# Moving the norm's root and shift behind the product: two extra columns, rows of 784 words, in a two-layer diffusion block

## The reference, cut to what matters

```python
def rms_norm(x, w):
    y = x * lax.rsqrt(jnp.mean(x * x, axis=-1, keepdims=True) + NORM_EPS) * w
def modulate(h, shift, scale):
    return h * (1.0 + scale) + shift
def swiglu(h, w_in, w_out):
    gate, up = jnp.split(h @ w_in, 2, axis=-1)
    return (jax.nn.silu(gate) * up) @ w_out

mod = (silu(c) @ w_ada[layer] + b_ada[layer])      # 9 vectors of 1024, one set for latent, one for context
h = h + 0.5 * lm[2] * swiglu(modulate(rms_norm(h, norm_w[layer, 0]), lm[0], lm[1]), ffn_w_in[layer, 0], ffn_w_out[layer, 0])
y, yc = token_mix(modulate(rms_norm(h, norm_w[layer, 1]), lm[3], lm[4]), ...)   # first product: @ w_in, 2048 columns
```

## Time and profile before

| | |
|---|---|
| time, median of 3 runs | 2741.3 us (2737.53 to 2744.84) |
| the profiled execution | 2739.12 us, of it the span 2737.2 us |
| mean granted TensorE clock | 0.992 |
| busy: PE / PEld / DVE / ACT / POOL | 2664.7 / 2290.5 / 1521.2 / 692.3 / 93.7 us |
| instructions in the span | 42267, of them 15515 matmuls |
| DMA read | 313.73 MB, 115 GB/s over the span |

### The profile page before, as it was taken

How to read it: one execution, slowest core, us unless ns; L and a number is a source line. 1 busy time by engine, 2 the same in 40 slices (tenths; PEclk the granted TensorE clock), 3 DMA queues, 4 the chain that set the end, 5 groups by cost and what they waited for, 6 DMA issues and landing times.

```text
span 2737.2 us, 42267 instructions
## 1 busy us (share of the span) xinstructions
PE 2664.7 (97%) x15515; PEld 2290.5 (84%) x15515; DVE 1521.2 (56%) x2621; ACT 692.3 (25%) x1075; POOL 93.7 (3%) x211
## 2 busy tenths in 40 slices
PE   7999999999999999999999999999999989999998
PEld 4888888888877888888888888888887877888886
DVE  5776477534376477626763677247536465543333
ACT  4111111122256221111111311111113345422222
POOL 0000000000034000000000000000000022000000
PEclk8999999999999999999999999999999999999999
DMA  7877477412200177536762577257422200233332
GB/s 228 198 184 185 113 184 184 125 50 79 54 17 2 54 165 185 146 86 159 184 161 58 123 184 175 71 140 184 126 70 84 69 26 17 81 96 100 91 110 81
DMA packets 485795, 316.98 MB, mean 116 GB/s; under 512 B 30588, under 2 KB 483664, under 8 KB 485712
## 3 DMA queue, kind: packets, MB, share of 16 engines
q1 hardware_dynamic: 485712, 315.88, 45.2%
HBM read 313.73 MB, written 2.10 MB: 115 GB/s over the span
## 4 chain that ended last, share of the span: by engine, by line
PE 91%; DVE 4%; ACT 2%; issue 1%; POOL 1%; DMA 0%; SPq 0%; DVEq 0%; ACTq 0%; POOLq 0%
PE pg L709 79%; PE pg L776 4%; PE p L1047 1%; PE pn L1030 1%; PE pg L986 1%; PE p L724 1%; DVE xlo L1640 1%; DVE tnorm L1632 1%; PE pg L867 1%; ACT whi L1155 0%; DVE wlo L1493 0%; PE pg L991 0%; DVE probT L1847 0%; DVE mx L1854 0%; ACT xhi L1244 0%
## 5 line engine op out<-in xcount | busy, mean ns | idle before, releaser
L709 PE MATMUL pg<-xhi,whi 128*128 128x512 f32 (+1 forms) x2856 | 794.5, 347 | 4.1 <-DVE wlo L1493 4.0
L709 PE MATMUL pg<-xhi,wlo 128*128 128x512 f32 (+1 forms) x2856 | 788.6, 344 | 0.0
L709 PE MATMUL pg<-xlo,whi 128*128 128x512 f32 (+1 forms) x2856 | 787.1, 344 | 0.0
L1155 ACT CAST whi<-raw 128x1024 fp32r<-128x1024 f32 (+1 forms) x288 | 321.8, 1118 | 1060.2 <-PE pg L709 1045.9
L1493 DVE TENSOR_TENSOR wlo<-raw,whi 128x1024 fp32r<-128x1024 f32 (+1 forms) x288 | 377.6, 1311 | 350.5 <-ACT whi L1155 347.8
L709 PEld LDWEIGHTS pg<-xhi,whi 128*128 128x128 f32 x2856 | 451.3, 188 | 72.6 <-DVE wlo L1493 5.9
L709 PEld LDWEIGHTS pg<-xlo,whi 128*128 128x128 f32 x2856 | 450.4, 188 | 69.3
L709 PEld LDWEIGHTS pg<-xhi,wlo 128*128 128x128 f32 x2856 | 450.4, 188 | 68.9
L1577 DVE SCALAR_TENSOR_TENSOR part<-ada,cond,part 128x256 f32<-128x256 f32 x960 | 465.3, 485 | 32.7
L1703 DVE SCALAR_TENSOR_TENSOR h<-pg,gcol,h 128x512 f32 (+1 forms) x118 | 71.4, 639 | 442.3 <-PE pg L709 437.5
L709 PE MATMUL pg<-ahi,whi 128*128 128x512 f32 x1100 | 306.1, 346 | 0.0
(11 more groups left out here) (212 smaller groups left out, 1983.4 us busy)
## 6 DMA issues: line engine op xcount, KB each, us to landing
ada<-in_w_ada SPq DMA_DIRECT2D x512, 256.0 KB, 4.2
raw<-in_ffn_w_in SPq DMA_DIRECT2D x176, 512.0 KB, 3.9
raw<-in_ffn_w_out SPq DMA_DIRECT2D x64, 704.0 KB, 4.5
raw<-in_w_in SPq DMA_DIRECT2D x24, 512.0 KB, 3.8
ada_first<-in_w_ada SPq DMA_DIRECT2D x8, 1024.0 KB, 11.9
raw<-in_w_in SPq DMA_DIRECT2D x16, 256.0 KB, 3.5
raw<-in_w_o SPq DMA_DIRECT2D x16, 256.0 KB, 2.8
raw<-in_w_o SPq DMA_DIRECT2D x32, 128.0 KB, 2.9
```

Source lines behind the costliest of these rows:

```text
L709: last = nc.tensor.matmul(pg[s][:, p0:p1], w[:, s, k], v[:, k, p0:p1], start=(k == 0 and n == 0), stop=(k == kt - 1 and n == 2))
L1155: nc.scalar.copy(whi[:, s, 0:nk], raw[:, s, 0:nk]).then_inc(s_whi[s], 1)
```

## The change

Norms 0, 1, 2 and 3 (`POST`) are applied after the product. `xhi`, `xlo` hold A·h, without r and s; two more columns of them (768, 769) hold s for latent and context. So the second matmul of each pair has 258 columns, and rows of `xhi`, `xlo` have 784 words. At the eviction DVE multiplies `pg[s]` by `rstd` and copies the two columns W^T s to `gbias`; ACT adds them as its bias. Norms 4 and 5 stay as they were. After the `out` phases before norms 1 and 3 (`EARLY_K` = 6) the tiles k = 0 to 5 are written during the last pair. In the opening the squares are taken from the token rows with an accumulated sum on ACT; DVE makes a diagonal of them (`ident` times `ssq`) for the same `square_sums`; PE has these ahead of the first modulation. In norm 1 `rstd` goes to `rstd_w`, since `rope_sb` is loaded over `rstd`, and that load also waits for the root.

```diff
+        XB, XW = TOK + 2, TOK + 16
-        xhi = place("xhi", [P, KD, TOK], f32r, start["xhi"])
+        xhi = place("xhi", [P, KD, XW], f32r, start["xhi"])
...
+        POST = (0, 1, 2, 3)
+        EARLY_K = {1: KD - 2, 3: KD - 2}
+        def product_columns(m, t):
+            return TOK + 2 if m in POST else t
...
                         if n == (6 if late_context(i) else 4):
                             sp.wait_ge(s_xn, xn_count(m, 1, KD - 1))
+                            sp.wait_ge(s_r, 2 * m + 2)
...
-                parts = [(0, SEQ)] + ([(SEQ, TOK)] if t == TOK else [])
+                parts = [(0, SEQ)] + ([(SEQ, t)] if t > SEQ else [])
...
-                        if part_ == 0 and (s, k) == (0, 1):
+                        if part_ == 0 and (s, k) == (order[-1] if m in POST else (0, 1)):
                             square_sums(m, 1)
...
             def opening_pair(i):
-                first_modulation(0)
                 square_sums(0, 0)
                 square_sums(0, 1)
+                first_modulation(0)
                 first_fold(0)
...
+            for tt in range(TOK // P):
+                act.wait_ge(s_x[tt // 2], 32)
...
+                nc.scalar.activation(sqjunk[tt % 2][:, :], xtok[:, tt, :], ACT.Square, accum_out=ssq[:, tt:tt + 1]
+                                     ).then_inc(s_sq, 1 if tt < TOK // P - 1 else KD - TOK // P + 1)
...
+            def scaled_hi(m, part_, k):
+                nc.scalar.activation(xhi[:, k, p0:p1], h[:, k, p0:p1], ACT.Identity, scale=acol[:, k, v:v + 1]
+                                     ).then_inc(s_xh, 1)
+            def shift_columns_hi(m, k0, k1):
+                nc.scalar.copy(xhi[:, k0:k1, TOK:XB], mod[:, shift + k0:shift + k1, 0:2])
...
+                if m == 0:
+                    for q in range(KD // 2):
+                        if q == 2:
+                            copy_first(2)
+                        act.wait_ge(s_coef, coef_count(0, 2 * q))
+                        shift_columns_hi(0, 2 * q, 2 * q + 2)
+                        for k in (2 * q, 2 * q + 1):
+                            scaled_hi(0, 0, k)
+                            scaled_hi(0, 1, k)
+                        if q == 1:
+                            nc.scalar.preload_act_table_set("natural_log_exp_and_others")
+                            root(0)
+                            root(1)
+                    return
+                if m in POST:
+                    if phases[i][0] == "wo":
+                        act.wait_ge(s_coef, coef_count(m, 0))
+                        for k in range(4):
+                            scaled_hi(m, 0, k)
+                        split_hi(i + 1, 0, 0)
+                        square_part(i, 1, 0)
+                        for k in range(4, KD):
+                            scaled_hi(m, 0, k)
+                        split_hi(i + 1, 1, 0)
...
+                        if m in POST:
+                            split_hi(nxt, 0, jn)
+                            act.wait_ge(s_free[0], read_value(i, f))
+                            nc.scalar.activation(gate[:, 0:SEQ], gate[:, 0:SEQ], ACT.Silu, bias=gbias[:, 0:1])
+                            nc.scalar.activation(gate[:, SEQ:TOK], gate[:, SEQ:TOK], ACT.Silu, bias=gbias[:, 1:2]
+                                                 ).then_inc(s_gd, 1)
+                            split_hi(nxt, 1, jn)
+                            return
...
+                        if m in POST:
+                            dve.wait_ge(s_unit[0], f + (j0 + 1))
+                            nc.vector.tensor_tensor(gate[:, :], pg[0][:, 0:TOK], rstd[:, :], ALU.mult)
+                            nc.vector.tensor_copy(gbias[:, 0:2], pg[0][:, TOK:XB]).then_inc(s_free[0], 1)
                         split_lo(nxt, 0, jn)
...
+                        if m in POST:
+                            nc.vector.tensor_copy(gbias[:, 2:4], pg[1][:, TOK:XB])
+                            nc.vector.tensor_tensor(u, pg[1][:, 0:TOK], rstd[:, :], ALU.mult).then_inc(s_free[1], 1)
+                            dve.wait_ge(s_gd, gate_count(m, hf, f))
+                            for v, (p0, p1) in enumerate(((0, SEQ), (SEQ, TOK))):
+                                last = nc.vector.scalar_tensor_tensor(gate[:, p0:p1], u[:, p0:p1],
+                                                                      gbias[:, 2 + v:3 + v], gate[:, p0:p1],
+                                                                      ALU.add, ALU.mult)
...
+                        if m in POST:
+                            nc.vector.tensor_tensor(z[:, n, :], pg[s][:, 0:TOK], rstd_w[:, :], ALU.mult)
+                            nc.vector.tensor_scalar(gbias[:, 2 * s:2 * s + 2], pg[s][:, TOK:XB], tile_scale(n), None,
+                                                    ALU.mult).then_inc(s_free[s], 1)
+                            split_lo(nxt, s, jn)
```

More of the change, by code:

```diff
@@ L125, in transformer @@
         h = place("h", [P, KD, TOK], f32, start["h"])
-        xhi = place("xhi", [P, KD, TOK], f32r, start["xhi"])
-        xlo = place("xlo", [P, KD, TOK], f32r, start["xlo"])
+        xhi = place("xhi", [P, KD, XW], f32r, start["xhi"])
+        xlo = place("xlo", [P, KD, XW], f32r, start["xlo"])
         ahi = place("ahi", [P, HALF, TOK], f32r, start["ahi"])
@@ L141, in transformer @@
         gate = place("gate", [P, TOK], f32, m0 + TOK * 4)
+        up = place("up", [P, HALF, TOK], f32, start["alo"])
+        gbias = sb("gbias", [P, 4])
+        sqjunk = [place(f"sqjunk{b}", [P, D], f32, at) for b, at in enumerate((m0 + 3 * TOK * 4, m0 + 4096))]
+        ssq = place("ssq", [P, TOK // P], f32, m0 + 3 * TOK * 4 + D * 4)
         xtok = place("xtok", [P, TOK // P, D], f32, start["alo"])
@@ L159, in transformer @@
               for tt in range(TOK // P)]
-        ysum = [place(f"ysum{ft}", [P, TOK], f32, start["xlo"] + ft * TOK * 4) for ft in range(2)]
-        ysin = [place(f"ysin{ft}", [P, TOK], f32, x0 + ft * TOK * 4) for ft in range(2)]
+        ysum = [place(f"ysum{ft}", [P, TOK], f32, start["xlo"] + ft * XS) for ft in range(2)]
+        ysin = [place(f"ysin{ft}", [P, TOK], f32, x0 + ft * XS) for ft in range(2)]
         vret = place("vret", [P, TOK // P, 2 * P], f32, m0)
         xlo0 = start["xlo"]
-        kdk = place("kdk", [P, TOK // P, RH, 2, HD], f32, xlo0 + 4 * TOK * 4)
-        qd = [place(f"qd{hd}", [P, TOK], f32, x0 + k * TOK * 4) for hd, k in enumerate((2, 3, 6, 7))]
+        kdk = place("kdk", [P, TOK // P, RH, 2, HD], f32, xlo0 + 4 * XS)
+        qd = [place(f"qd{hd}", [P, TOK], f32, x0 + k * XS) for hd, k in enumerate((2, 3, 6, 7))]
         qdt = place("qdt", [P, RH, P], f32, start["ada"] + 2 * TOK * 4)
@@ L1082, in _ @@
                         with pe.Fori(a, e) as f:
-                            unit(i, 0, f, xhi, xlo, t)
-                            unit(i, 1, f, xhi, xlo, t)
+                            unit(i, 0, f, xhi, xlo, product_columns(m, t))
+                            unit(i, 1, f, xhi, xlo, product_columns(m, t))
                             if b is not None:
@@ L1666, in norm @@
                         read_first(q)
-                        scaled(0, 2 * q)
-                        scaled(1, 2 * q)
-                        low(0, 2 * q)
-                        scaled(0, 2 * q + 1)
-                        low(1, 2 * q)
-                        scaled(1, 2 * q + 1)
+                        scaled_low(0, 0, 2 * q)
+                        shift_columns_low(0, 2 * q, 2 * q + 2)
+                        scaled_low(0, 1, 2 * q)
+                        scaled_low(0, 0, 2 * q + 1)
                         if q == 0:
                             copy_first(1)
-                        low(0, 2 * q + 1)
-                        low(1, 2 * q + 1)
+                        scaled_low(0, 1, 2 * q + 1)
+                    return
+                if m in POST:
+                    if phases[i][0] == "wo":
+                        for k in range(3):
+                            scaled_low(m, 0, k)
+                        add_part(i, 1, 0)
+                        split_lo(i + 1, 0, 0)
+                        scaled_low(m, 0, 3)
+                        sum_part(m, 1, 0)
+                        for k in (4, 5):
+                            scaled_low(m, 0, k)
+                        add_part(i, 1, 1)
+                        split_lo(i + 1, 1, 0)
+                        for k in (6, 7):
+                            scaled_low(m, 0, k)
+                        sum_part(m, 1, 1)
+                        shift_columns_low(m, 0, KD)
+                        for k in range(KD):
+                            scaled_low(m, 1, k)
+                    else:
+                        split_lo(i + 1, 0, 0)
+                        sum_part(m, 1, 0)
+                        add_part(i, 1, 1)
+                        scaled_low(m, 1, KD - 2)
+                        split_lo(i + 1, 1, 0)
+                        sum_part(m, 1, 1)
+                        scaled_low(m, 1, KD - 1)
```

(8 more changed lines are left out.)

185 lines of the change are left out of this document (135 added, 50 removed).

## The result

The kernel after takes 2750.35 us (median of 7 runs, 2749.2 to 2754.04), the kernel before 2741.3 us in the same comparison (2737.53 to 2744.84): **ratio 1.0033, 95% interval 1.0022 to 1.0044**. It is slower by 9 us, just past the 0.3% taken as the bound (the interval lies on both sides of it), where the forecast was 2725.5 us with a range to 2736. The profiled execution took 2749.2 us (span 2747.4). Every gain that was forecast is there, and more than their sum has gone into the pace of TensorE's products.

The account below looks back on a forecast made before the run. PE, busy in 97% of the span, was taken as the bound. Terms +3.0 − 5.5 − 4.4 − 5.6 − 3.4 − 0.5 + 0.6 gave −15.8 us, moving the median 2741.3 to 2725.5 us, range 2716 to 2736.

Parts of the forecast that it names:

- Norms 1, 2 and 3: Where these norms meet the next product, PE's waits for `xlo` tiles and splits shrink: −5.5, −5.6 and −4.4 us.
- the opening: Earlier sums of squares give −3.4 us, the opening pair −0.5; first product near 61.7 instead of 65.6.
- PE's clock no longer falls there: Sign at the norms: the forecast is wrong if the granted clock still falls at norms 1 and 2.
- the first mixing: ACT's query copies start some 0.6 us later, delaying DVE's decay product: +0.6 us, between 0 and 1.2.
- the eviction is hidden: In 132 FFN and 16 mixing units, DVE's added 2.5 us per step fits its idle time: 0 us.
- one gap left in the step: Sign in FFN steps: DVE idle about 1.3 us ahead of the up tile, under 0.5 ahead of slot 0's split.
- Rival D: DVE becomes the bound of the FFN steps, all 61 stretch by 0.4 us, +24 − 16: 2750 us; chance 0.06.
- the sign that I had set: The forecast is wrong if a steady FFN step is longer than 17.2 us; 17.14 expected instead of 17.10.
- Two more columns: 3552 second matmuls grow from 256 to 258 columns, 0.83 ns each: +3.0 us on PE, ends 0 and 3.5.
- Rival C: The two columns are free under the weight load: −18.8 us, 2722.5 us; chance 0.12.

Follow-up runs that it names:

- Run 14: Changed kernel with rows of 832 words and 256 columns in the second matmul, the shift left out of the products; 2722.26 us, ratio 0.9929.
- run 5: Changed kernel with rows of 800 words instead of 784, 258 columns kept; 2754.19 us, ratio 1.005.
- run 6: Changed kernel with rows of 784 words, but 256 columns instead of 258 in the second matmul; 2743.44 us, ratio 1.0011.
- run 7: Changed kernel with rows of 800 words and 256 columns in the second matmul; 2746.22 us, ratio 1.0021.
- run 13: Changed kernel with rows of 832 words, 258 columns kept; 2738.74 us, ratio 0.9998.
- Run 18: Changed kernel, 832-word rows, shift packed in `xhi`, order whi·xhi (260 columns), wlo·xhi (258), whi·xlo (256); 2716.95 us, ratio 0.9912.
- run 2: Kernel before with 512 bytes left free behind `xhi` and again behind `xlo`, rows still 768 words; 2740.69 us, ratio 0.9995.
- run 4: Kernel before with everything moved by 384 bytes together; 2741.14 us, ratio 1.0002.
- run 10: Kernel before with `xhi`, `xlo` moved by 256 bytes against everything else; 2739.46 us, ratio 0.9996.
- run 12: Kernel before with everything moved by 64 bytes together; 2741.91 us, ratio 1.0004.
- run 15: Kernel before with the opening's part of the change alone; 2739.45 us, ratio 0.9998.
- run 16: Changed kernel, 832-word rows, shift packed in `xhi`, order whi·xhi (260 columns), whi·xlo (256), wlo·xhi (258); 2742.42 us, ratio 1.0007.
- run 17: Changed kernel, 832-word rows, packed shift, only whi·xhi past 256 columns (260), wlo times the shift left out; 2728.76 us, ratio 0.9952.
- run 3: Kernel before with `xhi`, `xlo` moved by 64 bytes, rows of 768 words; 2771.25 us, ratio 1.0115.
- run 8: Kernel before with the weights `whi`, `wlo` moved by 64 bytes, all else in place; 2776.52 us, ratio 1.0129.
- run 11: Kernel before with `xhi`, `xlo` moved by 128 bytes against everything else; 2764.25 us, ratio 1.0086.

## Why the prediction was wrong

**Right, to within 0.7 us: what the order of the work gives.** Norms 1, 2 and 3 were to gain 5.5, 5.6 and 4.4 us and gained 5.5, 5.3 and 4.3; the opening 3.9 and 4.6 at the first product. PE's clock no longer falls there. In the first mixing ACT's first query copy now comes 2.30 us after the last product and came 1.77 after it, +0.5 where +0.6 stood. Run 14 has the whole change without columns and pitch: 18.3 us below before; the sum without the columns' 3.0 was −18.8. That this agrees so closely is partly luck: its four executions spread over 10.6 us, and in the profiled one the long rhythm takes 9.5 us in the first FFN while the x624 pieces give back 4.2.

**Right: the eviction is hidden.** VectorE has one gap left in the step, 2.07 us ahead of the up tile (forecast 1.3), none ahead of the split of slot 0 (forecast under 0.5), and is busy for 14.56 us of 17.40:

```profile
210.50 1.22 DVE L1606 TENSOR_TENSOR wlo<-raw,whi 128x1024 fp32r<-128x1024 f32 x1
211.65 4.12 DVE L1693 SCALAR_TENSOR_TENSOR part<-ada,cond,part 128x256 f32<-128x256 f32 x8
217.84 0.16 DVE L2071 COPY gbias<-pg 128x2 f32<-128x2 f32 x1 [2.07 <-PE pg L744]
```

Rival D, which forecast 2750 us for this reason, would have been right by its number and wrong by its cause: VectorE still waits for PE in every step. The step itself broke the sign that I had set, 17.40 us with its fold where 17.2 was the bound.

**Wrong: "Two more columns", +3.0 us with ends 0 and 3.5.** The slope from 256 to 512 columns was taken for the price of going from 256 to 258, and the step was excluded by the row of sixteen matmuls with 257 columns, 0.217 us each. Those run at nearly twice the time of a unit's matmul of 256 columns (0.120) and can't show 7 ns in the rhythm of units. The columns cost 5 to 8 us at rows of 784 and 800 words (runs 5 to 7) and 16.5 us by the medians at 832 (run 13 against 14), in the order in which the kernel issues its products. Rival C, free columns, rested on the rule of the Trainium skill, TensorE: Matmul & The Clock Gate, section on the back-to-back issue gap, that weight load and matmul set the spacing together. Run 18, whose steps have the short mean, is 0.02 us a step above 16.75; it is too near to both 0 and the slope's 0.04 to decide between them.

**Wrong by leaving it out: the row pitch.** "Rows of 784 words" stood in the change and nowhere in the sum. It costs 11.6 us with the columns (2750.35 against 2738.74 at 832 words), 21.2 without them (2743.44 against 2722.26), and 21.4 in the kernel before. The two rows of the trace that could have warned were there: the long rhythm in some stretches of the kernel before, 110.38 us for 624 matmuls beside 68.78 for 396. Per pair that is 353.8 and 347.4 ns, and no wait lies in either. I had read one pace and taken it for all.

The two prices don't add as separate terms. Columns first, they are 16.5 and 11.6 us; pitch first, 21.2 and 6.9. Either way 28.1 us stand where the sum had 3.0, and that is the 25 us by which the forecast was off. The −18.3 of run 14 and these 28.1 make +9.8 against a measured +9.0, but this is no test: the medians of runs 13 and 14 cancel in that sum. Times of different comparisons are good to 2 or 3 us here, since the kernel before had medians from 2739.4 to 2742.0.

**Open.** Why a distance of 64 or 128 bytes costs 16 periods, why rows that lie right are slowed too when the distance changes from k to k, why pairs have two rhythms and what lets a stretch take one or the other, why 258 columns cost more at one pitch than at another, and what the order of the products would give to the kernel before or to rows of 784 words; those two weren't tried. For the kernel before an estimate is at most 5.8 us: the long stretches of its chain (x624 twice, x288 and x192) hold 864 pairs, at 16 periods each.

## What to carry to other kernels

When a change alters the pitch or the place of a tensor that TensorE streams, price it like an instruction: choose start and pitch so that every distance to the weight tiles stays a multiple of 256 bytes, as with the 3072 and 3328 bytes here, and compare the length of a stretch whose instructions didn't change. Read the pace of back-to-back matmuls in several stretches of the trace before taking one for the price of a column, and try the order of the products where the pace has two values. Where an extra column is needed, let the fewest matmuls carry it, and measure it in the rhythm in which it will run.

## What the runs showed of the hardware

- The 512-column matmuls of this kernel follow one another at 226.7 ns (544 periods of 2.4 GHz) when every distance between weight tiles and rows is a multiple of 256 bytes (last FFN 348.5 us, runs 2, 4, 10 and 12 to 18), and at 233.3 ns (560 periods) when all are off by 64 or 128 (units of 5.60 us, runs 3, 8 and 11). Moving both together, by 64 or 384 bytes, changes nothing. With rows of 784 or 800 words the rows that lie right are slowed as well (units of 5.56 and 5.57 us).
- Pairs of 512 and 256 columns run at a mean of 346.7 or 353.3 ns where the distances are right. The difference is 16 periods a pair, and falls on the three pairs of a k as 350, 350 and 360 ns; a stretch keeps its rhythm over hundreds of matmuls. The `out` phase of 198 pairs took 68.8 or 70.1 us in every profile of the study, and nothing between.
- The order whi·xhi, wlo·xhi, whi·xlo gave the short mean in the steps and in all `out` stretches; whi·xhi, whi·xlo, wlo·xhi with the same columns gave the long one in the steps and in most of the `out` stretches (runs 18 and 16: 2716.95 and 2742.42 us). These two differ in nothing else.
